# First tap and bias of six convolution tiles moved from VectorE to ScalarE, and each silu one unit half later, in a two-layer hybrid decoder step

## The reference

```
def causal_conv(x, buf, w, b):
    xp = jnp.concatenate([buf, x], axis=1)
    l = x.shape[1]
    y = sum(xp[:, j:j + l] * w[j] for j in range(CONV_WIDTH)) + b
    return y, xp[:, -(CONV_WIDTH - 1):]
xbc, conv_new = causal_conv(xbc, conv_buf, p['ssd_conv_w'], p['ssd_conv_b'])
xbc = jax.nn.silu(xbc)
xc, conv_new = causal_conv(xb, conv_buf, p['lru_conv_w'], p['lru_conv_b'])
```

## Time and profile before

| | |
|---|---|
| time, median of 3 runs | 1489.09 us (1482.39 to 1490.59) |
| profiled execution, its own time | 1478.99 us |
| its span | 1477.2 us |
| PE busy | 1428.3 us (97%) |
| DVE busy | 709.0 us (48%) |
| ACT busy | 448.0 us (30%) |
| POOL busy | 376.9 us (26%) |
| mean granted TensorE clock | 0.968 of full speed |
| PE's share of the chain that ended last | 82% |
| DVE's share of it | 10% |

### The profile page before, as it was taken

One profiled execution on the slowest core, in us unless ns is written; L12 is line 12 of the kernel. 1 busy time (PEld: TensorE's weight loads), 2 busy tenths in 40 slices (PEclk: granted clock), 3 DMA queues, 4 the chain that ended last, 5 costly groups with the idle time before them and its releaser, 6 DMA issues.

```text
span 1477.2 us, 26393 instructions
## 1 busy us (share of the span) xinstructions
PE 1428.3 (97%) x11529; PEld 1374.9 (93%) x11529; DVE 709.0 (48%) x1302; ACT 448.0 (30%) x605; POOL 376.9 (26%) x161
## 2 busy tenths in 40 slices
PE   6999999999999999999998999999999999999996
PEld 6888878899999999999998887889999999999996
DVE  6845868454331333123767566764643213321334
ACT  5414224333221222122442151434422212222231
POOL 1000000243344443333500000003333333344441
PEclk9999989899999999999999998989999999999998
DMA  6212221122222222222322122121222222222231
GB/s 225 73 51 81 71 69 44 62 100 85 87 86 86 86 87 86 90 92 91 103 82 72 44 87 83 44 76 61 83 87 86 88 90 93 87 86 87 86 98 64
DMA packets 35012, 123.35 MB, mean 84 GB/s; under 512 B 4433, under 2 KB 5457, under 8 KB 34769
## 3 DMA queue, kind: packets, MB, share of 16 engines
q1 hardware_dynamic: 30528, 112.33, 23.5%
q10 hardware_dynamic: 4368, 9.34, 2.1%
HBM read 113.60 MB, written 5.82 MB: 81 GB/s over the span
## 4 chain that ended last, share of the span: by engine, by line
PE 82%; DVE 10%; DVEq 3%; ACT 2%; issue 1%; DMA 1%; ACTq 0%; POOL 0%; SPq 0%
PE bank L1172 72%; DVE wl L1060 1%; DVE ct L706 1%; PE bank L1125 1%; PE bank L1359 1%; PE bank L1381 1%; PE bank L1214 1%; DVEq L945 1%; PE bank L1369 0%; PE bank L1315 0%; PE bank L1350 0%; PE bank L1243 0%; DVEq L894 0%; PE bank L1141 0%; PE bank L1200 0%
## 5 line engine op out<-in xcount | busy, mean ns | idle before, releaser
L1172 PE MATMUL bank<-xh,wh 128*128 128x272 f32 x2208 | 657.9, 298 | 17.1 <-DVE xl L663 7.6
L370 POOL TENSOR_TENSOR wl<-raw,wh 128x1024 fp32r<-128x1024 f32 x157 | 376.7, 2400 | 1074.3 <-ACT wh L394 1058.5
L1172 PE MATMUL bank<-xh,wl 128*128 128x272 f32 x2208 | 649.2, 294 | 0.0
L1172 PE MATMUL bank<-xl,wh 128*128 128x272 f32 x2208 | 645.7, 292 | 0.0
L1172 PEld LDWEIGHTS bank<-xh,wh 128*128 128x128 f32 x2208 | 427.1, 193 | 29.9 <-issue 22.3
L1172 PEld LDWEIGHTS bank<-xl,wh 128*128 128x128 f32 x2208 | 427.6, 194 | 0.7
L1172 PEld LDWEIGHTS bank<-xh,wl 128*128 128x128 f32 x2208 | 426.0, 193 | 0.0
L394 ACT ACTIVATE wh<-raw 128x1024 fp32r<-128x1024 f32 x199 | 210.6, 1059 | 699.1 <-PE bank L1172 692.1
L1094 DVE TENSOR_TENSOR tz<-bank,rs_bcast 128x272 f32<-128x272 f32 x176 | 77.5, 442 | 293.4 <-PE bank L1172 289.0
L1074 DVE TENSOR_TENSOR h<-h,bank 128x272 f32<-128x272 f32 x128 | 55.4, 436 | 215.3 <-PE bank L1172 215.3
L1172 PE MATMUL bank<-gh_gla,wh 128*128 128x272 f32 x256 | 73.9, 289 | 1.0 <-DVE gl_gla L1102 1.0
(11 more groups left out here) (305 smaller groups left out, 1796.9 us busy)
## 6 DMA issues: line engine op xcount, KB each, us to landing
raw<-weights SPq DMA_DIRECT2D x202, 512.0 KB, 3.5
h<-x SPq DMA_DIRECT2D x4, 544.0 KB, 6.0
y<-h SPq DMA_DIRECT2D x4, 544.0 KB, 2.8
cs<-consts SPq DMA_DIRECT2D x1, 1597.0 KB, 9.6
rv<-rk ACTq DMA_DIRECT2D x8, 136.0 KB, 2.5
tz<-rq ACTq DMA_DIRECT2D x8, 136.0 KB, 2.4
S<-s_ssd ACTq DMA_DIRECT2D x2, 512.0 KB, 4.3
n_ssd<-Vx ACTq DMA_DIRECT2D x2, 512.0 KB, 3.0
```

The costliest lines, as they stand in the source:

```text
L370: nc.gpsimd.tensor_tensor(wl[:, s, :], raw[:, s, :], wh[:, s, :].bitcast(F32), ALU.subtract).then_inc(lo_done, 1)
L1172: ins = mm(bank_, wt[:, n % RING, w], xx[:, cols], start=(i == 0 and j == 0), stop=(i == len(ks) - 1 and j == 2))
```

## The change

The first tap with the bias becomes one ScalarE activation, `Identity(scale * row + bias)`, in the tile's odd slot behind `hi_ahead`. Two semaphores carry the new hand-overs: `conv_row` from VectorE's drain behind lines 693 and 694, and `conv_tap` from the activation back to VectorE. VectorE does `split` first and then the three taps that remain. ScalarE's silu of a tile moves from the tile's odd slot to the start of the next even slot, so behind the stages of the odd slot.

```
@@ ScalarE @@
+                def first_tap(t):
+                    act.wait_ge(conv_row.sem, conv_row.at(layer, t + 1))
+                    a(conv_target(t), cbuf[:, t % 3, 0:CW], ACT.Identity, scale=conv_weight(t, 0),
+                      bias=par("ssd_conv_b", t) if t < 4 else par("lru_conv_b", t - 4)).then_inc(conv_tap.sem, 1)
                 for s in range(2 * NIN):
                     u = s // 2
+                    if s % 2 == 0 and u and IN_UNITS[u - 1][0] == "xbc":
+                        silu_conv(u - 2)
                     if s % 2:
                         name = IN_UNITS[u][0]
                         if u < NIN - 1:
                             hi_ahead(layer, u)
-                        if name == "xbc":
-                            silu_conv(u - 1)
+                        if name in ("xbc", "lx"):
+                            first_tap(u - 1)
@@ VectorE @@
-                    dve.drain()
+                    dve.drain().then_inc(conv_row.sem, 1)
                     copy(conv_out[:, t, 0:3], row[:, SEQ:SEQ + 3])
                     copy(conv_out[:, t, 3:27].rearrange("p (b l) -> p b l", b=NSEQ), samples(row, 4, 3))
-                    w, b = ("ssd_conv_w", par("ssd_conv_b", t)) if t < 4 else ("lru_conv_w", par("lru_conv_b", t - 4))
-                    out = (ct[:, t % 2, :] if t < 4 else lru_x[:, t - 4, :])[:, 0:CW]
-                    if 2 <= t < 4:
-                        dve.wait_ge(conv_silu.sem, conv_silu.at(layer, t - 1))
-                    ts(out, row[:, 0:CW], par(w, 4 * (t % 4)), b, ALU.mult, ALU.add)
+
+                def later_taps(t):
+
+                    row, out = cbuf[:, t % 3, :], conv_target(t)
+                    dve.wait_ge(conv_tap.sem, conv_tap.at(layer, t + 1))
                     for j in range(1, 4):
-                        dve.drain()
-                        ins = stt(out, row[:, j:j + CW], par(w, 4 * (t % 4) + j), out, ALU.mult, ALU.add)
+                        ins = stt(out, row[:, j:j + CW], conv_weight(t, j), out, ALU.mult, ALU.add)
+                        if j < 3:
+                            dve.drain()
                     ins.then_inc(conv_done.sem, 1)
@@ VectorE, slots @@
                     evacuate(s // 2, s % 2)
                     if s % 2 and s // 2 + 2 in ON_VECTOR:
                         split(s // 2 + 2)
+                    if s % 2 and IN_UNITS[s // 2][0] in ("xbc", "lx"):
+                        later_taps(s // 2 - 1)
```

More of the change, by code:

```diff
@@ L294, in trunk @@
         dt_ready = signal("dt_ready", 1)
-        conv_done = signal("conv_done", 6)
+        conv_row, conv_tap, conv_done = signal("conv_row", 6), signal("conv_tap", 6), signal("conv_done", 6)
         conv_silu = signal("conv_silu", 4)
@@ L332, in dense_bank, with conv_target, conv_weight @@
             return (M[BORROWED[q]] if q in BORROWED else dense[(layer * (2 * NUNIT) + q) % 3])[:, 0:HALF]
+        def conv_target(t):
+            return (ct[:, t % 2, :] if t < 4 else lru_x[:, t - 4, :])[:, 0:CW]
+        def conv_weight(t, j):
+            return par("ssd_conv_w" if t < 4 else "lru_conv_w", 4 * (t % 4) + j)
         def by_sequence(cols):
```

## The result

The changed kernel took 1472.37 us (median of 9 runs, 1470.22 to 1476.71), the kernel before 1482.39 us in 9 runs beside them (1480.29 to 1490.59). The ratio is 0.9930, 95% interval 0.9908 to 0.9952: 10.0 us or 0.7% faster. The forecast was 1484.3, a gain of 4.8 on a base of 1489.09. Of the miss of 11.9 us, 6.7 is that base, a median of three runs of which two lay high (in 28 runs of the kernel before it was 1481.5), and 5.2 is the size of the change.

A forecast was written before the change was run, and what follows sets the result against it. VectorE was taken as the bound over the six tiles heading each input projection; -1.6 us (layer 0) and -3.2 (layer 1), clock nothing, gave -4.8 from 1489.09: 1484.3 us. Range 1476 to 1492 (8 in 10), likeliest case 1479 to 1489.

The forecast's parts named there:

- The likeliest case: Whole kernel: the forecast of 1484.3 us, 4.8 us gained, own range 1479 to 1489, chance 0.50.
- The first rival: Whole kernel: the clock or TensorE's lead give more, both low stretches may go, -8.2 to -9.2 us, 1480; chance 0.20.
- First tap gone from VectorE: VectorE, six tiles of each layer: 0.66 us saved per tile with its drain, -3.96 us a layer.
- My wait at tile 2: Tile 2: VectorE waits 2.46 us for ScalarE's late first tap, +2.45 us a layer, the largest new cost.
- dt's wait: VectorE's wait for `dt`: the Exp table load is hidden behind tile 1's first tap, -0.65 us a layer.
- Tiles 1 and 3: Loop between ScalarE and VectorE: VectorE waits 0.24 us each time; +0.6 us in layer 0, +0.5 in layer 1.
- Layer 1's slack for TensorE's sake: Layer 1, lines 789 and 693: VectorE's idles of 0.65 and 0.90 us for TensorE vanish, -1.55 us.
- TensorE's new idles: TensorE waits about 2.1 us at `ssd_b(0)`, where it did not before, and 1.2 us at line 1200, in layer 1.
- The sum of the chain: VectorE's chain from tile 0 to line 1200: -1.6 us in layer 0 and -3.2 us in layer 1.
- I take one such low stretch as before: nothing: TensorE's clock: one low stretch, 3.4 us lost in layer 0 before, was assumed to recur, so no gain.
- Nothing is left: First taps of 0.95 us, slower hand-overs and waits at all six tiles cost 3.2 us: 1487.5 to 1489; chance 0.17.
- The slower case: Tile 2: table switches stall ScalarE about twice their load, 1492.0 us, or 1498.8 with the clock; chance 0.13.

The follow-up runs named there:

- idle_back: The changed kernel with one wait more: TensorE starts half 10 only when VectorE has emptied half 8; 1480.12 us, ratio 0.9978 to the kernel before.
- idle_at_ssd: The change with tile 1's silu and tiles 4 and 5's later taps moved later, plus TensorE's `ssd_a(1)` waiting for tile 5's taps; 1474.50 us, ratio 0.9953.
- before_taps_late: The kernel before, all four taps on VectorE, those of tiles 4 and 5 put behind `ssd_a(0)` and `ssd_b(0)`; 1476.37 us, ratio 0.9960.
- split_last: The changed kernel with VectorE's order undone: the three later taps ahead of `split`; 1491.08 us, ratio 1.0055 to the kernel before.

## Why the prediction was wrong in size: the chain held, the clock did not

The chance for "faster" was 0.28, the range began at 1476.0, and the time lay below it. The likeliest case was not the one that came. The first rival was, in sign and nearly in size ("both low stretches named may go": 8.2 to 9.2 us; measured 10.0), with a chance of 0.20.

**First tap gone from VectorE.** Held: 12 instructions fewer, each replaced on ScalarE. The activation's price was mis-sized, 0.76 taken, 0.85 and 0.86 measured. The nearest row had one pointer operand, this one has two. The 0.05 for the semaphore came from no row of before; measured is 0.03 (the tap ends at 52.75, VectorE starts at 52.78). My wait at tile 2 came out right all the same: 2.46 forecast, 2.36 and 2.02 measured.

**dt's wait.** Held: 1.09 fell to 0.31, about 0.5 forecast.

**Tiles 1 and 3.** Held: 0.24 forecast, 0.15 and 0.16 measured.

**Layer 1's slack for TensorE's sake, and TensorE's new idles.** Held: VectorE's idles of the earlier trace rows are gone, TensorE waits 1.68 at `ssd_b(0)` (2 forecast) and 1.2 at `ssd_a(1)` (1.2 forecast).

**The sum of the chain.** -1.05 and -3.34 against -1.6 and -3.2: 0.4 us off in all. Layer 0 fell short by 0.55, and an issue gap of 0.49 us at tile 1 (at 41.00) that nothing in the trace explains is most of it. Layer 1 profited from the like: there the kernel before had such a gap of 0.43 us (at 762.03) and the change has none. That the total comes out to 0.4 is partly luck.

**The term that failed** is "I take one such low stretch as before: nothing". I had counted low stretches and idles in one execution, found the low clock behind the idle of 1.81 but not behind that of 1.85, and took it to come after the change as often as before. With the step from 1.8 to 1.2 us at the same place, in front of the same small matmuls, it went: none is left in the 12 layers of the six kernels with 1.2 us or less there and no wait added, where the two executions of before had three behind `ssd_a(1)` and three more among the tiles, in four layers. In its place the runs showed a mean clock of 0.971 instead of 0.966, by the slope some 6 us, which is the 5 to 6 us beyond the chain. That an idle brings such a stretch was shown by adding one (idle_back, idle_at_ssd), and before_taps_late, which shortens the idle at `ssd_a(1)` and leaves those on the split, raised the mean clock from 0.966 to 0.969. Not shown is which stretches the median gained. The lost clock that went from these stages is 5.1 us in the first execution of before and 10.2 in the second, but the total of the first, 47 us, is also that of the change's first execution, where others of the same size stand elsewhere. Nor is it shown which idle brought those among the tiles: the change shortened several at once.

**The base.** I put the sum on the median of three runs, though the profiled execution and the lowest of the three, 1482.39, said that it lay high.

**The rivals that fell.** "Nothing is left" needed waits at every tile; they were not there. The slower case rested on a table switch that costs twice its load. The loads at 43.51 and 47.09 above, and the one in the earlier trace rows, are followed by the next activation within 0.02 us. The Trainium skill's drain of 1380 ns (ScalarE: Activation LUTs, "What ACT_TABLE_LOAD costs") is not seen at any of them; the measurement decides. But the place from which a loss would come was rightly named: more lateness of ScalarE at tile 2 goes to the end. split_last has it by another way, with 3.48 us of wait, TensorE idle 4.84, and a loss of 9.6 us.

**Open.** Why the same kernel at 1.8 us of idle has the low stretch in some executions only; and the lost clock further back, in the stages behind the first 30 us, about 17 us in each layer (10 to 22), in kernels of both kinds. It spreads from one execution to the next by more than the 5 to 6 us in question, so that only many runs show the change's gain in clock.

## What to carry to other kernels

Moving one link of a bound engine's chain to another engine pays when work that is independent stands between the hand-over and the wait: here one split of 1.13 us made the difference between 0.7% faster and 0.55% slower. Cost TensorE's idles twice, once as time and once as the clock that may follow, and look at more than one execution before calling a low stretch chance; here a gain in mean clock as large as that of the whole chain came with an idle that shrank from 1.8 to 1.2 us ahead of a stage of small matmuls. Compare two kernels at the same mean clock to see what the chain alone gives. Before the work is moved, try moving what is not urgent: putting two tiles' taps behind the stage that TensorE waits for gave 0.4% alone and, on top of the change with one silu moved too, made the best kernel (0.9875).

## What the runs showed of the hardware that was not expected

- The two profiled executions of the kernel before, same code, differ by 9.9 us, at mean granted clocks of 0.968 and 0.961.
- Low stretches are between the chip's two levels in the mean (0.57 to 0.84 in windows of 8 to 20 us, where 0.50 is 1.2 GHz throughout and 1.00 is 2.4 GHz), each 1.7 to 7 us of lost clock. At `ssd_a(1)` there was one at an idle of 1.8 us in four of six cases and at one of 2.37 us or more in all four; at tile 0 there was one at the idle of 2.50 us in ten of twelve.
- An Identity of 128x568 with pointers for scale and bias takes 0.848 us (0.862 into `lru_x`), a Tanh of the same shape with a pointer scale alone 0.756. The difference of 0.09 us is put down to the second pointer; no run here changes the pointer alone. The Trainium skill (ScalarE: Activation LUTs, "What ACT_TABLE_LOAD costs") has 93 ns for each pointer operand on top of 186 ns and 0.833 ns an element, which gives an estimate of 845 ns here; the trace agrees.
